# The last expert pairs placed by one-hot products in two pieces, and the other pairs' rows summed by GpSimd

## What is computed

```python
def hierarchical_moe(xn, ...):          # t = 256 tokens, 32 experts, TOP_K = 2
    ...
    top_v, top_i = lax.top_k(e_in, TOP_K)
    top_p = jax.nn.softmax(top_v, axis=-1) * g_w        # the gates, one per token and choice
    ...
    def expert_block(args):
        xb, e = args
        hb = jax.nn.silu(xb @ w_g[e]) * (xb @ w_u[e])   # 1024 -> 512
        return hb @ w_d[e]                              # 512 -> 1024
    ...
    y = y_pad[dest] * gates[order][:, None].astype(y_pad.dtype)
    out = jnp.zeros((t, d), xt.dtype).at[token_idx[order]].add(y)
```

## Time and profile before

| | us |
|---|---|
| median of 3 runs | 1832.05 |
| the runs | 1828.74, 1832.05, 1832.53 |
| the profiled execution, as measured | 1828.17 |
| its span in the trace | 1826.3 |
| busy: TensorE, VectorE, ScalarE, GpSimd | 1786.6, 1289.4, 1032.3, 107.6 |

### The profile page before, as it was taken

How to read it: one execution, slowest core, us unless ns; L and a number is a source line. 1 busy time by engine, 2 the same in 40 slices (tenths; PEclk the granted TensorE clock), 3 DMA queues, 4 the chain that set the end, 5 groups by cost and what they waited for, 6 DMA issues and landing times.

```text
span 1826.3 us, 22533 instructions
## 1 busy us (share of the span) xinstructions
PE 1786.6 (98%) x9265; PEld 1513.9 (83%) x9265; DVE 1289.4 (71%) x1293; ACT 1032.3 (57%) x1067; POOL 107.6 (6%) x107
## 2 busy tenths in 40 slices
PE   8998999999999999999999999999999999999998
PEld 7987888887888787788899888888888899888886
DVE  6876799999999998655478655555554777755554
ACT  5554688889898886544344454435443544444442
POOL 1010211101010100000000000000000100000000
PEclk9999999999999999999999999999999999999999
DMA  9842789999999999555464355546554754446550
GB/s 349 257 153 104 296 344 404 413 390 414 406 409 413 409 412 367 196 184 188 147 253 159 138 179 187 193 168 218 186 185 161 275 186 158 167 161 220 184 191 38
DMA packets 69916, 450.26 MB, mean 247 GB/s; under 512 B 11299, under 2 KB 11671, under 8 KB 18608
## 3 DMA queue, kind: packets, MB, share of 16 engines
q1 hardware_dynamic: 59744, 425.44, 61.9%
q0 software_dynamic: 9856, 22.78, 4.0%
q10 hardware_dynamic: 208, 0.54, 0.1%
HBM read 448.50 MB, written 14.16 MB: 253 GB/s over the span
## 4 chain that ended last, share of the span: by engine, by line
PE 82%; DMA 7%; DVE 6%; ACT 3%; issue 2%; POOL 0%; ACTq 0%; POOLq 0%; SPq 0%; DVEq 0%
PE PS L492 22%; PE PS L494 22%; PE PS L493 22%; PE PS L1644 8%; DMA ring<-in_wt 6%; PE PS L1650 2%; DVE wl L470 2%; DVE morel L470 1%; PE PS L2263 1%; ACT wh L461 1%; PE PS L1635 1%; PE PS L2789 1%; PE PS L531 1%; ACT yr L1994 1%; ACT us L1971 0%
## 5 line engine op out<-in xcount | busy, mean ns | idle before, releaser
L470 DVE TENSOR_TENSOR wl<-ring,wh 128x2048 fp32r<-128x2048 f32 (+1 forms) x345 | 782.1, 2279 | 290.7 <-ACT wh L461 290.0
L461 ACT ACTIVATE wh<-ring 128x2048 fp32r<-128x2048 f32 (+1 forms) x345 | 657.2, 1908 | 299.9 <-PE PS L494 269.4
L492 PE MATMUL PS<-wh,XTh 128*128 128x512 f32 x952 | 378.7, 398 | 7.6 <-DVE XTl L595 2.9
L494 PE MATMUL PS<-wh,XTl 128*128 128x512 f32 x952 | 371.9, 391 | 0.0
L493 PE MATMUL PS<-wl,XTh 128*128 128x512 f32 x952 | 371.6, 390 | 0.0
L492 PEld LDWEIGHTS PS<-wh,XTh 128*128 128x128 f32 x952 | 179.1, 188 | 45.5 <-DVE wl L470 4.0
L494 PEld LDWEIGHTS PS<-wh,XTl 128*128 128x128 f32 x952 | 179.1, 188 | 38.3
L493 PEld LDWEIGHTS PS<-wl,XTh 128*128 128x128 f32 x952 | 179.4, 188 | 35.3 <-issue 0.2
L1644 PE MATMUL PS<-wh,xgT 128*128 128x512 f32 x384 | 154.9, 403 | 0.0
L1644 PE MATMUL PS<-wl,xgT 128*128 128x512 f32 x384 | 150.8, 393 | 0.0
L492 PE MATMUL PS<-wh,hTh 128*128 128x512 f32 x352 | 137.6, 391 | 0.0
(11 more groups left out here) (443 smaller groups left out, 2556.2 us busy)
## 6 DMA issues: line engine op xcount, KB each, us to landing
ring<-in_wt SPq DMA_DIRECT2D x389, 1024.0 KB, 6.8
park<-in_wt SPq DMA_DIRECT2D x9, 1024.0 KB, 6.9
xtmp<-in_norm_g POOLq DMA_DIRECT2D x6, 512.0 KB, 5.1
ring<-in_wt SPq DMA_DIRECT2D x4, 512.0 KB, 7.6
toep<-frow POOLq DMA_DIRECT2D x1, 2048.0 KB, 55.0
y_d<-in_zero POOLq DMA_DIRECT2D x1, 2048.0 KB, 38.5
yy<-y_d POOLq DMA_DIRECT2D x4, 512.0 KB, 5.8
bv<-in_b_b_in POOLq DMA_DIRECT2D x1, 1536.0 KB, 9.0
```

The source lines that it names most:

```text
L461: s.activation(k.pieces(i)[0], k.raw(i), ACT.Copy).then_inc(*k.w_hi.up(i))
L470: v.tensor_tensor(l, k.raw(i), h.bitcast(F32), ALU.subtract).then_inc(*k.w_lo.up(i))
L492: pe.matmul(o, lhsT=left[0], rhs=right[0], start=first, stop=False)
L494: return pe.matmul(o, lhsT=left[1], rhs=right[0], start=False, stop=final)
```

## The change

- Pairs 14 and 15 both stay on the chip. Their rows are multiplied with the seat's gate and cut in two float32r pieces, `yh` by ScalarE (`final_rows`) and `yl` by VectorE (`row_low`). `PT` is now 0 or 1, one for each pair, and 16 float32r products (`combine`) place them.
- The gate of each seat comes to its partition through HBM: GpSimd stores the 512 gates and gathers them with the scatter's indices (`gates_gpsimd`, within pair 8's turn). `gm`, `hotg`, and the products with ones go.
- GpSimd scatters pairs 0 to 13, reads `y_d` back when these have landed, multiplies each `yy` by its gates and adds it to X: eight `tensor_tensor` of 128x1024. VectorE's four additions go.
- ScalarE waits for the last of GpSimd's additions (`xy1.1`) before it writes the rows of pair 15, since `yh1` and `yl1` lie where `yy` lay. TensorE waits for `yl0.1` before the down product of expert 30.
- SyncE no longer waits for `yy`.
- The fourth weight buffer begins one part later. With that, the first two parts of f0 follow on the two down parts of expert 30, and their splits now stand ahead of the last pair's rows on ScalarE and VectorE.

```diff
@@ Kernel.__init__ @@
-            len(self.parts), ((self.at["co"], n_end), (self.at["a_out"], self.at["a_out"])))
+            len(self.parts), ((self.at["co"] + 1, n_end), (self.at["a_out"], self.at["a_out"])))
@@ experts_tensor @@
-            pe.wait_ge(*m.s.at(f"yb{e // 2 - 1}"))
+            pe.wait_ge(*(m.v.at("yl0.1") if e == 30 else m.s.at(f"yb{e // 2 - 1}")))
...
-        if e == 10:
-            pe.wait_ge(*m.v.at("hotg"))
-            for x in T:
-                for t in T:
-                    mm = pe.matmul(bank(6, 128, 256 * x + 128 * t), lhsT=k.ones, rhs=k.hotg[:, x, t, :], start=True,
-                                   stop=True)
-            mm.then_inc(*m.pe.up("gates"))
...
     down(30)
+    down(31)
+
+    def combine(x, t, nn):
+
+        for y in (k.yh, k.yl):
+            mm = pe.matmul(bank(COMBINED[2 * t + nn]), lhsT=k.PT[x][:, 128 * t:128 * t + 128],
+                           rhs=y[x][:, 512 * nn:512 * nn + 512], start=x == 0 and y is k.yh, stop=x == 1 and y is k.yl)
+        return mm
+
     pe.wait_ge(*m.v.at("PT1"))
-    down(31)
+    for nn in T:
+        combine(0, 0, nn)
     for t in T:
         for nn in T:
-            if t == 0:
-                pe.wait_ge(*m.s.at(("ya15", "yb15")[nn]))
-            pe.matmul(bank(COMBINED[2 * t + nn]), lhsT=k.PT[:, 128 * t:128 * t + 128],
-                      rhs=k.yr[:, 1, 512 * nn:512 * nn + 512], start=True, stop=True).then_inc(
-                *m.pe.up(f"c{t}.{nn}"))
+            if t:
+                combine(0, t, nn)
+            pe.wait_ge(*m.v.at(f"yl1.{nn}"))
+            combine(1, t, nn).then_inc(*m.pe.up(f"c{t}.{nn}"))
@@ experts_vector @@
+    def row_low(x):
+
+        for nn in T:
+            o = slice(512 * nn, 512 * nn + 512)
+            v.wait_ge(*m.s.at(f"y{'ab'[nn]}{14 + x}"))
+            if x == 0:
+                v.wait_ge(*k.d["yd1"].at(13))
+            v.scalar_tensor_tensor(k.yl[x][:, o], bank(4 + nn), k.seat_gate[:, x:x + 1], k.yh[x][:, o].bitcast(F32),
+                                   ALU.mult, ALU.subtract).then_inc(*m.v.up(f"yl{x}.{nn}"))
...
+        if e == 30:
+            row_low(0)
...
-    for t in T:
-        for q, gate in ((0, k.st[:, 0:2]), (1, k.st[:, 2:4])):
-            v.wait_ge(*k.d["yy"].at(3))
-            if q:
-                v.wait_ge(*m.v.at(f"xy{t}.0"))
-            v.scalar_tensor_tensor(k.X[:, t, :], k.yy[2 * q + t], gate[:, t:t + 1], k.X[:, t, :], ALU.mult,
-                                   ALU.add).then_inc(*m.v.up(f"xy{t}.{q}"))
+    for i in k.at["down", 30]:
+        split_lo(v, k, k.after[i])
+    row_low(1)
@@ gates_vector @@
...
     for x in T:
-        for t in T:
-            v.tensor_scalar(k.hotg[:, x, t, :], k.ident, k.gm[:, t, x:x + 1], None, ALU.mult).then_inc(
-                *m.v.up("hotg" if x and t else f"hotg{x}.{t}"))
+        v.tensor_scalar(k.PT[x], k.places, k.tok[:, x:x + 1], None, ALU.is_equal).then_inc(*m.v.up(f"PT{x}"))
@@ experts_scalar @@
+    def final_rows(x):
+
+        s.wait_ge(*k.d["sg"].at(1))
+        s.wait_ge(*(m.g.at("xy1.1") if x else k.d["yd0"].at(12)))
+        for nn in T:
+            s.wait_ge(*(m.pe.at("y31") if (x, nn) == (1, 0) else k.w_used.at(k.at["down", 29 + 2 * x][1])))
+            s.activation(k.yh[x][:, 512 * nn:512 * nn + 512], bank(4 + nn), ACT.Copy,
+                         scale=k.seat_gate[:, x:x + 1]).then_inc(*m.s.up(f"y{'ab'[nn]}{14 + x}"))
...
-    rows(15)
+    for i in k.at["down", 30]:
+        split_hi(s, k, k.after[i])
+    final_rows(1)
@@ experts_gpsimd @@
-    for j in range(15):
+    for j in range(14):
         g.wait_ge(*m.pe.at(f"xt{j + 1}.1g"))
         if j + 3 < 16:
             gather(g, k, j + 3)
+        if j == 8:
+            gates_gpsimd(g, k)
...
-    for j in (13, 14):
+
+    for j in (12, 13):
         g.wait_ge(*k.d[f"yd{j % 2}"].at(j))
+    g.wait_ge(*k.w_lo.at(k.at["moe"] + 22))
     for q in range(4):
         g.dma_start(k.yy[q], k.y_d[128 * q:128 * q + 128, :]).then_inc(*k.d["yy"].up(q))
+    g.wait_ge(*k.d["yy"].at(3))
+    for q in T:
+        for t in T:
+            n = 2 * q + t
+            g.tensor_tensor(k.yy[n], k.yy[n], k.st[:, n:n + 1].broadcast_to([128, 1024]), ALU.mult).then_inc(
+                *m.g.up(f"yg{t}.{q}"))
+            g.wait_ge(*m.g.at(f"yg{t}.{q}"))
+            if q:
+                g.wait_ge(*m.g.at(f"xy{t}.0"))
+            g.tensor_tensor(k.X[:, t, :], k.X[:, t, :], k.yy[n], ALU.add).then_inc(*m.g.up(f"xy{t}.{q}"))
+
+
+def gates_gpsimd(g, k):
+
+    m = k.moe
+    g.memset(k.seat_gate, 0.0).then_inc(*m.g.up("sg"))
+    g.wait_ge(*m.v.at("gd"))
+    g.dma_start(k.gate_d.rearrange("(c p) o -> p (c o)", p=128), k.st[:, 0:4], allow_slow_non_contiguous=True).then_inc(*k.d["gt"].up("gt"))
+    g.wait_ge(*m.g.at("sg"))
+    g.wait_ge(*k.d["gt"].at("gt"))
+    for x in T:
+        g.indirect_dma_start(out=k.seat_gate[:, x:x + 1], out_offset=None, in_=k.gate_d,
+                             in_offset=bass.IndirectOffsetOnAxis(ap=k.six[:, 14 + x:15 + x], axis=0), bounds_check=511,
+                             oob_is_err=False).then_inc(*k.d["sg"].up(x))
@@ moe_end_vector @@
-    v.wait_ge(*m.v.at("xy1.1"))
+    v.wait_ge(*m.g.at("xy1.1"))
...
     entered(0, 1)
-    split_lo(v, k, k.after[a])
     enter_low(v, k, k.f0, 0, 0)
-    split_lo(v, k, k.after[b])
@@ sync_program @@
-        if i == k.at["f0"]:
-            sp.wait_ge(*k.d["yy"].at(3))
         load_part(sp, k, i)
```

## The result

| | before | after |
|---|---|---|
| median, runs of the comparison | 1830.57 (4 runs, 1828.74 to 1832.53) | 1847.27 (4 runs, 1846.22 to 1848.47) |
| ratio to before | | 1.0095, 95% interval 1.0083 to 1.0106 |
| span of the profiled execution | 1826.3 | 1844.4 |
| f0's first matmul on TensorE | 721.57 | 741.41 |
| from there to the end of the span | 1104.7 | 1103.0 |

The changed kernel is 0.95% slower, 16.7 us by the medians, near the 16.1 of the prediction. f0's first matmul is 19.8 us later; 1.7 us come back behind it. The sum came out nearly right, but its terms did not: the gates cost time instead of giving some back, and the reads and GpSimd's arithmetic differ in size, as the trace shows place by place.

What follows compares the result with a forecast made beforehand. Weight transfers set the experts' pace, VectorE second by a hair. Gates -1.0, lateness at the last split +19.4, shorter path to f0 -2.3: +16.1 us on the median 1832.05, so 1848.2, range 1829 to 1855.

Steps and rivals of the forecast that it cites:

- gates: At 365 us: dropping VectorE and TensorE gate work gains 1.0 us, between -1.4 and +1; GpSimd's store and gathers are covered.
- reads: Before the experts' end: four y_d reads, 2.10 MB, in the full DMA stretch delay VectorE's weights by 4.8 us (0 to 5.1).
- GpSimd's arithmetic and pair 14, less idle time: From 683 us: eight GpSimd operations cost VectorE 14.4 us (0 to 20.8), pair 14's two operations 1.4, less 1.2 idle.
- last split to f0: From the last expert split's end to f0's first matmul: 10.0 us instead of 12.33, a gain of 2.3.
- The bound of +1: Upper end of the -1.0 us term at 365 us; up to 2 us lost if small pieces hold up weight transfers.
- the very sign that the prediction had named: If the two pairs around 365 us still take 64 us, the gates' term was wrong.
- Half the bandwidth, over at 683: The y_d reads, issued from about 673 us, get half the DMA bandwidth and are over at about 683 us.
- the half of the lock that the trace showed: GpSimd's one-column power operation, 0.55 us as a rule, took 2.54 and 2.58 when a VectorE split_lo had just begun.
- rival A: Experts' end: GpSimd's reads do not hold VectorE up; -0.2 us, median 1832, or 1830 if the clock stays up; chance 0.16.
- SyncE's wait: Before f0's weights: its removal brings nothing by itself, since f0's splits stood behind VectorE's queue, not behind a landing.
- B: As rival A, but the reads fit between the weights (0 instead of 4.8): -4.0 us, median 1828; chance 0.10.
- C: Experts' end: VectorE keeps the interface, GpSimd starves until about 720 us, pair 15's rows wait; +15 to +23, median about 1851; chance 0.12.

## Why the prediction was right in the sum, and not in its terms

| term, shift of f0's start | predicted | in the trace |
|---|---|---|
| gates | -1.0 | +4.5 (-1.3 ahead of the store, +6.1 across it, -0.3 behind; the first and the last within chance) |
| reads | +4.8 | +6.0 (alone: 5.8, and 1.5 by TensorE's stops) |
| GpSimd's arithmetic and pair 14, less idle time | +14.6 | +11.4 |
| last split to f0 | -2.3 | -2.0 |
| sum (of unrounded terms) | +16.1 | +19.8 |
| behind f0's start | 0 | -1.7 |

- **The gates** are the step that failed. The prediction had the case in view ("If their many small pieces hold up the weight transfers, up to 2 us are lost") and took the cover, 27 us of rest on GpSimd's queue, for an answer. The cover was real: nobody waited for the store. But the path went through the DMA engines, which the same prediction had called full, and 512 pieces took more of them than any count of bytes says. The bound of +1 was never worked out from a row. Nor did the gain of 1.0 come: two pairs still take 64.7 us around 365 us on average, 64.5 before, the very sign that the prediction had named for this term being wrong. Over all traces pair 13's scatter stands at 669.5 us on average in the six with the 4-byte store and the gathers, and at 664.0 in the five without a store: +5.5 rather than the +4.5 of this one pair of executions.
- **The reads** stood where they were expected (677.27 = 673 and the gates' lateness) and held up the weights by 6.0 us for 4.8. Half the bandwidth, over at 683, was wrong: they got a third of it and landed at 696.9, so that GpSimd's arithmetic began 14 us later than in the prediction, 4.5 of these from the gates. It still found enough splits to hold up.
- **GpSimd's arithmetic** is confirmed in kind: the prediction took the half of the lock that the trace showed and assumed the other, and three variants (only writing: all of it gone; half the operations: half; none: 10.0 back) show the price at the last split at 10 to 11 us. In the kernel's time less is seen to come back, and only with the memsets does it nearly stand clear of the noise. The operation by itself is 2.07 us, the 2.1 worked out from memset and the smallest operation; the 2.25 estimated from the Trainium skill ("GPSIMD Engine Reference", Performance versus the Vector engine) lies above. The size: eight times 2.07 are 16.6 us, which held VectorE for 12.0; the first operation ran while VectorE waited for weights, another beside `row_low`. The first of these was not in the sum.
- **The tail** was right, 10.3 us for 10.0. That TensorE's clock loss of the earlier trace rows would go was set down only in rival A; it went here: in the window around f0's start the granted clock is 1.00 for the 0.83 of the earlier trace rows, where eight matmuls in a row took 0.43 us from start to start instead of 0.23. These 1.7 us come back.

```profile
740.00:750.00 10.00, 9.17 (x46) 7.47 (x47) 5.92 (x9) 5.45 (x8) 0.00 (x0) 1.00 0.03 12
```

- **SyncE's wait** "brings nothing by itself" was right for this change and wrong as a reason: in this change the reads are over at 696.89, while SyncE issues f0's first part only at 713.86, so the wait would not have held anything (read from the trace; no run has the wait put back there). In the three kernels in which it would have, its absence costs 9.6 (with the split moved as well), 10.1 and 11.7 us by the medians.
- **The rivals.** A and B fell with the drawn-out splits. C did not come: `final_rows(1)` starts at 733.52, 7 us behind the last addition's end at 726.41. In A's sum the 1.4 us of pair 14's two operations were forgotten, which would have made it +1.2 instead of -0.2.

That 16.1 met 16.7 is partly luck. The terms came out 3.7 larger; 1.7 came back behind f0, and the profiled execution of before lay 2.4 under its median, that of after 1.0 under its own, which takes another 1.4 off.

## What to carry to other kernels

Before work goes to an idle GpSimd, ask what it reads: beside a VectorE that always has two SBUF inputs, eight operations of 2 us on the idle engine cost the full one 10 to 11 us up to its last split, while writes and one-input operations pass. Price a small transfer in a full DMA stretch by its pieces (their number or their size), not by its bytes or by who waits for it. And a wait on the load queue that looks like lost time can be a priority: what it holds back is what nobody can use yet.

## What the runs showed of the hardware

- 2 KB from SBUF to HBM in 512 pieces of 4 bytes brought the DMA engines down to 84 to 102 GB/s for a window of 5 us at a share of 0.67 to 1.02; in 128 pieces of 16 bytes to 353 GB/s.
- Four reads of 512 KB from GpSimd's queue beside SyncE's full one landed 16.6 to 19.6 us after their issue, one 1 MB part of the weights coming in 3.76 us, two thirds of 417 GB/s; with SyncE held, 8.6 to 8.7.
- `tensor_tensor` of 128x1024 on GpSimd with both inputs in SBUF: 2.07 us alone; on VectorE the like operation, 1.3. With a split under way GpSimd's takes 3.9 to 4.4, and VectorE's splits beside it up to 4.45 instead of 2.29. Beside 20 memsets of the same size on GpSimd, 0.96 to 0.99 us each, no split took over 2.30.
- TensorE stopped for 2.8 us between 496 and 499 us; from 500 to 505 us its granted clock was 0.50, the lower of its two levels, 1.2 GHz, while it was busy the whole time.
